# Window attention with fused mask-and-minimum sums, and the delta rule's decay rows from one pass over all chunks

## The reference, cut to what matters

```
G = jnp.cumsum(gc, axis=-1)
diff = G[..., :, None] - G[..., None, :]
dec_incl = jnp.where(incl, jnp.exp(jnp.where(incl, diff, 0.0)), 0.0)
...
t_mat = eye + bc[..., :, None] * dec_strict * kk
w_mat = triangular_solve(t_mat, ...)
```

```
s_loc = where(|i - j| <= 128, q k^T * scale, -1e30)
s_ctx = q k_ctx^T * scale
p = softmax(concat([s_loc, s_ctx, s_sink]))
o = p[..., :n_loc] v + p[..., n_loc:] v_ctx
```

## Time and profile before

| | |
|---|---|
| median of 3 executions | 3681.94 us (3679.02 to 3684.13) |
| the profiled execution | 3679.53 us, of which the span is 3677.7 us |
| PE busy | 3455.9 us (94% of the span) |
| DVE busy | 1802.4 us (49%) |
| ACT busy | 1175.1 us (32%) |
| POOL busy | 693.2 us (19%) |

### The profile page before, as it was taken

One profiled execution on the slowest core, in us unless ns is written; L12 is line 12 of the kernel. 1 busy time (PEld: TensorE's weight loads), 2 busy tenths in 40 slices (PEclk: granted clock), 3 DMA queues, 4 the chain that ended last, 5 costly groups with the idle time before them and its releaser, 6 DMA issues. The chain is left out here.

```text
span 3677.7 us, 49398 instructions
## 1 busy us (share of the span) xinstructions
PE 3455.9 (94%) x19822; PEld 2656.2 (72%) x19822; DVE 1802.4 (49%) x3343; ACT 1175.1 (32%) x2057; POOL 693.2 (19%) x528
## 2 busy tenths in 40 slices
PE   7999999999999999999976767988999999999998
PEld 6767778878888888875545656556887478888886
DVE  4277971233785554345577884678211243223222
ACT  3276751222211111234434453158111131112110
POOL 1190000110101111010020110048001213333333
PEclk9999999999999999999988887999999999999999
DMA  3101111121233322113012124000123011111111
GB/s 136 38 2 41 41 49 44 58 96 53 92 98 101 100 92 81 63 51 126 1 27 44 35 48 140 18 1 2 43 75 102 4 58 58 46 46 46 58 46 46
DMA packets 266352, 211.84 MB, mean 58 GB/s; under 512 B 65680, under 2 KB 231184, under 8 KB 265744
## 3 DMA queue, kind: packets, MB, share of 16 engines
q1 hardware_dynamic: 264368, 201.61, 17.7%
q10 hardware_dynamic: 1760, 7.08, 0.9%
HBM read 185.33 MB, written 21.50 MB: 56 GB/s over the span
## 5 line engine op out<-in xcount | busy, mean ns | idle before, releaser
L95 PE MATMUL ps<-halves 128*128 128x512 f32 x10408 | 2407.3, 392 | 18.4 <-DVE halves L1546 6.6
L95 PEld LDWEIGHTS ps<-halves 128*128 128x128 f32 x10408 | 1954.7, 188 | 441.3 <-issue 28.3
L95 PE MATMUL ps<-arena 128*128 128x512 f32 (+1 forms) x880 | 367.9, 572 | 8.0 <-issue 3.4
L1525 POOL TENSOR_TENSOR tmps<-tmps 128x512 f32<-128x512 f32 x128 | 143.9, 1124 | 979.6 <-ACT tmps L1493 979.6
L1546 DVE TENSOR_TENSOR halves<-tmps,halves 128x512 fp32r<-128x512 f32 x128 | 89.0, 698 | 432.2 <-ACT halves L1501 432.2
L1429 ACT ACTIVATE halves<-raws 128x2048 fp32r<-128x2048 f32 x62 | 118.4, 1909 | 554.8 <-PE ps L95 532.4
L95 PEld LDWEIGHTS ps<-arena 128*128 128x128 f32 x880 | 165.9, 193 | 168.4 <-issue 157.3
L1532 POOL TENSOR_TENSOR arena<-arena 128x512 f32<-128x512 f32 x128 | 164.7, 1294 | 191.4 <-DVE arena L1573 191.4
L1493 ACT ACTIVATE tmps<-ps 128x512 f32<-128x512 f32 x128 | 76.6, 598 | 363.7 <-PE ps L95 353.7
L1573 DVE TENSOR_TENSOR arena<-ps,arena 128x512 f32<-128x512 f32 x128 | 87.7, 690 | 194.9 <-PE ps L95 188.4
L1369 DVE SCALAR_TENSOR_TENSOR arena<-arena,sc 128x128 f32<-128x128 f32 x448 | 163.3, 365 | 15.9
(11 more groups left out here) (303 smaller groups left out, 3235.7 us busy)
## 6 DMA issues: line engine op xcount, KB each, us to landing
raws<-in_w_ff SPq DMA_DIRECT2D x31, 1024.0 KB, 6.7
raws<-in_w_mlp SPq DMA_DIRECT2D x31, 1024.0 KB, 5.2
mixw<-in_w_in SPq DMA_DIRECT2D x56, 512.0 KB, 3.8
arena<-in_w_ada SPq DMA_DIRECT2D x48, 512.0 KB, 3.9
arena<-in_w_in SPq DMA_DIRECT2D x5, 2048.0 KB, 12.0
arena<-in_x SPq DMA_DIRECT2D x8, 1024.0 KB, 8.4
h_stash<-arena SPq DMA_DIRECT2D x1, 5120.0 KB, 30.5
inverses<-arena ACTq DMA_DIRECT2D x20, 256.0 KB, 2.9
```

The lines of the kernel that those rows point to most:

```text
L95: ins = e.matmul(out_ap, l, r, start=i == 0, stop=i == n - 1)
L1525: e.tensor_tensor(tt, tt, tt, ALU.mult).then_inc(*f_sq.tick())
```

## The change

The change has two parts. **In the window attention** DVE's two mask additions, its copy and its two maxima become four fused instructions: each adds the mask (or a row of zeros for the context columns), writes the negated sum and keeps the minimum, which starts from the negated sink for the local columns and from the local minimum for the context columns. The comparison with the sink (L2893) goes, as does ACT's copy of head 1 (L2916). ACT's exponentials take the negated scores with scale -1. POOL scales head 0 only; DVE scales head 1, right behind its reciprocal. The last transposes of a unit wait for both. **In the delta rule** POOL's gate products go. In conv turn 6 instead of 9, PE makes the running sums of all blocks at once as rows (80 partitions, 256 columns, bank `("sr",)`); ACT and DVE split them into a high and a low part (`GH`, `GL`); SP writes both to DRAM and reads them back as 20 rows of 1024 each into `GR`, which POOL has zeroed; `tensor_decay_rows` then picks one row by a selector column of `E2`, with a float32r matmul in place of the float32 one. `scalar_decay_rows` takes over the waits that POOL had. The scratch `sq` of the conv stage moves to another place.

```diff
@@ -1785,6 +1785,9 @@
+            e.wait_ge(*b_ab.at(1))
+            e.tensor_copy(GC_.rearrange("p (d t h) -> p t d h", d=2, t=10),
+                          ga3.rearrange("p t (d h) -> p t d h", d=2)).then_inc(*b_ab.tick())
@@ -1792,7 +1795,7 @@
-        sq = R3(CB, 10, 128)
+        sq = R3(F0 + 14336, 10, 128)
@@ -1802,7 +1805,7 @@
-        DECAYS, CHUNK0 = 9, 9
+        DECAYS, CHUNK0 = 6, 9
@@ -1921,6 +1924,7 @@
+                    scalar_decay_parts(e)
@@ -2001,6 +2005,7 @@
+                    vector_decay_parts(e)
@@ -2048,7 +2053,13 @@
-        e_gg, e_sv, e_ex = C("delta_gates"), C("delta_small"), C("delta_small_exp")
+        e_gg, e_sv, e_ex = C("decay_parts"), C("delta_small"), C("delta_small_exp")
+        l_gr = LD("decay_rows")
+        g_rows = nc.dram_tensor("decay_rows", [2, 2, 10, 8, 128], F32, kind="Internal").ap()
+        GC_ = R(CB + 1072, 160)
+        E2 = RR[:, CB + 1664:CB + 1696]
+        GH, GL = RR[0:80, CB + 560:CB + 816], RR[0:80, CB + 816:CB + 1072]
+        GR = RR[:, CB + 2048:CB + 3072].rearrange("p (j s i) -> p j s i", j=4, s=2)
@@ -2085,6 +2096,43 @@
+            key = ("sr",)
+            o = bk.open(key, e_ev)
+            e.wait_ge(*bk.vacant(key))
+            e.wait_ge(*b_ab.at(3))
+            for dd in range(2):
+                ins = e.matmul(o[0:80, dd * 128:dd * 128 + 128], GC_[:, dd * 80:dd * 80 + 80], cum[:, dd, :], start=True, stop=True)
+            ins.then_inc(*bk.filling(key))
+        def vector_decay_parts(e):
+            e.tensor_tensor(E2, ident[:, 0:32], ident[:, 32:64], ALU.add).then_inc(*e_gg.tick())
+            e.wait_ge(*e_gg.at(2))
+            e.tensor_tensor(GL, bk.tile(("sr",))[0:80, 0:256], GH.bitcast(F32), ALU.subtract).then_inc(*bk.emptying(("sr",)))
+        def scalar_decay_parts(e):
+            e.wait_ge(*e_gg.at(1))
+            e.wait_ge(*bk.full(("sr",)))
+            e.activation(GH, bk.tile(("sr",))[0:80, 0:256], ACT.Copy).then_inc(*e_gg.tick())
+        def sync_decay_parts(e):
+            e.wait_ge(*bk.clear(("sr",)))
+            for part in range(2):
+                e.dma_start(g_rows[part].rearrange("d t h i -> (t h) d i"),
+                            (GH, GL)[part].bitcast(F32).rearrange("p (d i) -> p d i", d=2)
+                            ).then_inc(*l_gr.tick())
+            e.wait_ge(*l_gr.at(2))
+            e.wait_ge(*s_zero.at(1))
+            for part in range(2):
+                e.dma_start(RR[32 * part:32 * part + 20, CB + 2048:CB + 3072].bitcast(F32),
+                            g_rows[part].rearrange("d t h i -> (d t) (h i)")).then_inc(*l_gr.tick())
+        def gpsimd_decay_rows(e):
+            e.wait_ge(*bk.clear(("mask",)))
+            e.wait_ge(*bk.clear(("sg",)))
+            e.wait_ge(*bk.clear(("sr",)))
+            e.memset(RR[:, CB + 2048:CB + 3072].bitcast(F32), 0.0).then_inc(*s_zero.tick())
@@ -2113,26 +2161,16 @@
-        def gpsimd_gates(e, n, dd):
-            if n >= 10:
-                return
-            g = AB[:, ORDERS[dd][n], dd * 8:dd * 8 + 8].rearrange("p (j s) -> p s j", s=2)
-            if n >= 3:
-                e.wait_ge(*(bk.full(("so", n - 3, dd)) if latent(n - 3, dd) else bk.clear(("kk", n - 3, dd, 1))))
-            for s in range(2):
-                ins = e.tensor_tensor(IT[n % 3][dd][:, s * 4:s * 4 + 4, :], bc(g[:, s, :].unsqueeze(2), [P, 4, 128]),
-                                      bc(cum[:, dd, :].unsqueeze(1), [P, 4, 128]), ALU.mult)
-            ins.then_inc(*e_gg.tick())
         def tensor_decay_rows(e, n, dd, s):
-            e.wait_ge(*e_gg.at(turn[n, dd] + 1))
+            e.wait_ge(*l_gr.at(4))
-            chain(e, o[:, :], [(ones, IT[n % 3][dd][:, s * 4:s * 4 + 4, :]),
+            c = dd * 10 + ORDERS[dd][n]
+            chain(e, o[:, :], [(bc(E2[:, c:c + 1], [P, 128]), GR[:, :, s, :]),
@@ -2142,6 +2180,10 @@
+            if n < 3:
+                e.wait_ge(*bk.full(("ci", 11, 1024) if n else ("ci", 7, 512)))
+            else:
+                e.wait_ge(*(bk.full(("so", n - 3, dd)) if latent(n - 3, dd) else bk.clear(("kk", n - 3, dd, 1))))
@@ -2618,28 +2660,21 @@
         def gpsimd_delta(e):
-            e.wait_ge(*b_ab.at(2))
-            e.wait_ge(*l_cum.at(1))
-            e.wait_ge(*bk.full(("ci", 7, 512)))
-            for dd in BOTH:
-                gpsimd_gates(e, 0, dd)
+            gpsimd_decay_rows(e)
-            gpsimd_gates(e, 1, 0)
-            gpsimd_gates(e, 1, 1)
-                gpsimd_gates(e, n + 2, 0)
-                gpsimd_gates(e, n + 2, 1)
         def sync_delta(e):
+            sync_decay_parts(e)
@@ -2781,7 +2816,8 @@
-        w_mx, w_ex, w_rc, w_sl = C("watt_max"), C("watt_exp"), C("watt_recip"), C("watt_scaled")
+        w_mx, w_ex = C("watt_max"), C("watt_exp")
+        w_rc, w_sl = C("watt_recip_and_second_scaled"), C("watt_first_scaled")
@@ -2806,7 +2842,7 @@
-                            bk.open(key, w_et if key[0::2] == ("wc", 1) else w_es)
+                            bk.open(key, w_es)
@@ -2821,6 +2857,8 @@
+                        if c0 + n4 > nt:
+                            e.wait_ge(*w_rc.at(2 * u + 2))
@@ -2861,6 +2899,8 @@
         def vector_watt(e):
+            e.tensor_scalar(nsk, sk, -1.0, None, ALU.mult).then_inc(*dv.tick())
+            e.wait_ge(*dv.now())
@@ -2880,19 +2920,19 @@
-                        e.tensor_tensor(z[:, s, 0:nl], bk.tile(("wl", i, s))[:, 0:nl], wn[:, m0:m0 + nl],
-                                        ALU.add).then_inc(*bk.emptying(("wl", i, s)))
-                    e.wait_ge(*bk.full(("wc", i, 0)))
-                    e.tensor_copy(z[:, 0, nl:nl + 256], bk.tile(("wc", i, 0))[:, 0:256]
-                                  ).then_inc(*bk.emptying(("wc", i, 0)))
+                        e.tensor_tensor_reduce(out=z[:, s, 0:nl], in0=bk.tile(("wl", i, s))[:, 0:nl],
+                                               in1=wn[:, m0:m0 + nl], scale=-1.0, scalar=nsk[:, j + 4 * s:j + 4 * s + 1],
+                                               op0=ALU.add, op1=ALU.min, accum_out=c[:, 4 + s:5 + s]
+                                               ).then_inc(*bk.emptying(("wl", i, s)))
-                        e.wait_ge(*bk.clear(("wc", i, s)))
-                        e.tensor_reduce(c[:, s:s + 1], z[:, s, 0:nl + 256], AX.X, ALU.max,
-                                        negate=True).then_inc(*dv.tick())
-                    e.wait_ge(*dv.now())
-                    e.scalar_tensor_tensor(out=c[:, 0:2], in0=sk[:, j:8:4], scalar=-1.0, in1=c[:, 0:2], op0=ALU.mult,
-                                           op1=ALU.min).then_inc(*dv.tick())
-                    e.wait_ge(*dv.now())
+                        e.wait_ge(*bk.full(("wc", i, s)))
+                        e.wait_ge(*bk.clear(("wl", i, s)))
+                        e.tensor_tensor_reduce(out=z[:, s, nl:nl + 256].rearrange("p (a b) -> p a b", a=2),
+                                               in0=bk.tile(("wc", i, s))[:, 0:256].rearrange("p (a b) -> p a b", a=2),
+                                               in1=bc(wn[:, 128:256].unsqueeze(1), [P, 2, 128]), scale=-1.0,
+                                               scalar=c[:, 4 + s:5 + s], op0=ALU.add, op1=ALU.min,
+                                               accum_out=c[:, s:s + 1]).then_inc(*bk.emptying(("wc", i, s)))
+                    e.wait_ge(*bk.clear(("wc", i, 1)))
@@ -2901,20 +2941,15 @@
+                    n, j, lo, hi = watt_pair(u)
+                    p = pp_[u % 4][:, 1, 0:(hi - lo) * 128 + 256]
+                    e.wait_ge(*w_rc.at(2 * u + 1))
+                    e.tensor_scalar(p, p, c[:, 7:8], None, ALU.mult).then_inc(*w_rc.tick())
         def scalar_watt(e):
-                if i < 32:
-                    n, j, lo, hi = watt_pair(i)
-                    nl = (hi - lo) * 128
-                    if i >= 4:
-                        e.wait_ge(*watt_turned(i - 4))
-                    key = ("wc", i, 1)
-                    e.wait_ge(*bk.full(key))
-                    e.activation(pp_[i % 4][:, 1, nl:nl + 256], bk.tile(key)[:, 0:256],
-                                 ACT.Copy).then_inc(*bk.emptying(key))
@@ -2924,7 +2959,7 @@
-                                           accum_out=c[:, 2 + s:3 + s])
+                                           scale=-1.0, accum_out=c[:, 2 + s:3 + s])
@@ -2943,11 +2978,9 @@
-                e.wait_ge(*w_rc.at(i + 1))
-                for s in range(2):
-                    p = pp_[i % 4][:, s, 0:w]
-                    ins = e.tensor_scalar(p, p, w4[i % 4][:, 6 + s:7 + s], None, ALU.mult)
-                ins.then_inc(*w_sl.tick())
+                e.wait_ge(*w_rc.at(2 * i + 1))
+                p = pp_[i % 4][:, 0, 0:w]
+                e.tensor_scalar(p, p, w4[i % 4][:, 6:7], None, ALU.mult).then_inc(*w_sl.tick())

```

More of the change, by code:

```diff
@@ L2267, in sync_inverses @@
             if n == 0:
-                e.wait_ge(*s_zero.at(1))
+                e.wait_ge(*s_zero.at(2))
             for dd in range(2):
@@ L2393, in tensor_step_a @@
             else:
```

(4 more changed lines are left out.)

## The result

The changed kernel takes **3653.07 us** (median of 4 runs, 3647.21 to 3657.74) against 3683.03 (3679.02 to 3687.69): ratio 0.9917, 95% interval 0.9898 to 0.9937, so 23 to 38 us won and 30 in the middle. The forecast was 3662, the range 3652 to 3674. The time lies at the range's edge, on the fourth rival's value (3655), to which I had given 0.07: the turns of the window attention fell to PE's own length. The forecast's own range, 3655 to 3668, missed it by 2 us. So the direction was right and the likeliest case was not.

The account below looks back on a forecast made before the run. PE was taken to bound the conv stage, DVE the delta stage and window attention. Window attention 11.7 plus delta rule 8.1 gave 19.8 us off the profiled 3679.5, 2.4 under the median 3681.9: 3662, range 3652 to 3674.

Parts of the forecast that it names:

- the fourth rival: Window attention: the turns fall to PE's 3.78 us, 27 us won in all, time 3655; chance 0.07.
- DVE's turn falls by 0.36 to 3.95: Window attention: DVE loses 3.12 us a turn and gains 2.76; held by PE, 0.30 a turn is counted.
- The second rival: Window attention: fused instructions or DVE's scaling cost their upper ends, 0.68, 0.53 or 0.77; turns win nothing, 3672; chance 0.15.
- the prediction's lower bound: Window attention's worst case: 32 x (3.12 - 3.37) + 2.1, so 6 us lost.
- the turns of the eight smaller units I count alike: Window attention: the smaller units win the same per turn, so 32 x 0.30 = 9.6 us.
- The end: Window attention's end: POOL's last scaling finishes at 2566.8 instead of 2568.97, so mixing starts 2.1 us sooner.
- The detour's cost in the conv stage: Conv turn 6: two more float32 products on PE for the new rows cost 0.5 us; the rest is hidden.
- The second inverse: Delta stage: five DVE operations there shrink from 4.51 us to 1.3, 3.2 won.
- The later collisions: Delta stage, three later turns: DVE's first operations no longer collide with POOL, 3.1 us won.
- that rival: Delta stage: blocks through DRAM, not DVE, set the pace and the waits keep the gain; 3670; chance 0.10.
- 2.9 in sum, of which I take 2.3: Before the first delta block: L2251, L2248 and the pair L1964 are no longer stretched, 2.3 us counted.
- The port rival: Window attention: POOL's scaling, if first, shuts out DVE's for 1.87 us a turn; time 3722; chance 0.06.

Follow-up runs that it names:

- watt_alone: The kernel before with only the window attention's part of the change; 3661.18 us, ratio 0.9943.
- delta_alone: The kernel before with only the delta rule's part of the change; 3675.84 us, ratio 0.9976.
- the ten profiles: Profiles of kernels with the changed delta rule, two such kernels left out; mean delta stretch 600.1 us against 608.3 with the old rule.
- f32_product: The changed kernel with the decay product run as float32 instead of float32r; 3656.8 us.
- both_pool: The changed kernel with both heads' probability scalings back on POOL; 3661.1 us.
- first_and_last: The changed kernel with DVE scaling the second head only for the first unit and the last four, POOL for those between; 3656.5 us.
- late_rows: The changed kernel with the decay rows made in conv turn 9, right ahead of their first use, instead of turn 6; 3658.3 us.
- hybrid: The changed kernel with DVE scaling the second head only from unit 28 on, POOL before that; 3654.2 us.

## Why the prediction was right, and where it was wrong

**The window attention: 11.7 forecast, 20.8 measured.** The step that failed is "DVE's turn falls by 0.36 to 3.95", with the 0.30 a turn counted from it. The turn fell by 0.55, to 3.76. The next bound was named and sized rightly (PE's 3.78); what was too long is DVE's side. The four fused instructions take 1.88 and not 2.08: I had put the accumulator's read, 0.08 each, on top of the addition's time, and it overlaps the next instruction. The scaling costs 0.47 and not 0.58. Together 0.31 less, of which the own waits took 0.14 back (0.12 behind the last fused one and 0.12 ahead of the scaling, against 0.10). The second rival, the upper ends, falls by the same figures. (The 3.37 in the prediction's lower bound is more than its own terms give, 2 x 0.68 + 2 x 0.53 + 0.77 + 0.10 = 3.29; with that the bound is some 3 lost and not 6.) So DVE's turn ends at 3.765, in a tie with PE, and the fourth rival came about with DVE at its floor too. The second fault is "the turns of the eight smaller units I count alike" with nothing for the filling. There 17.2 us became 11.8. That DVE's and POOL's shorter work counts whole while the first three units pass through with nothing beside them is my reading, not tried by itself. PE's wait ahead of the first transposes shrank from 4.38 to the 1.72 shown above. The kernel before, PE there (timeline):

```profile
2441.17 1.94 PE L2826 MATMUL ps<-identm,arena 128*128 128x128 f32 x8 [4.38 <-DVE arena L2883]
2443.04 2.51 PE L2813 MATMUL ps<-arena 64*128 64x384 f32 x8
```

Those transposes took 1.94 instead of 1.07, the scores 2.51 instead of 1.69: PE's clock was down there. But the clock is not what the sum rests on: in `watt_alone` it fell behind the same wait of 1.72, and the window stretch is the same. Filling 5.4 and units 15.4 make the 20.8; between `delta_alone` and `watt_alone`, where the filling trades with the first turns, it is 2.4 and 17.6. The end was right, 2.1 forecast: from the last reciprocal's end to the mixing stage's first product 9.87 us became 8.05, 1.8 less (2564.72 to 2574.59, 2543.54 to 2551.59).

**The delta rule: 8.1 forecast, 7.0 in the profile of after, 8.2 over the ten profiles.** The sum was right, but by luck: two of its terms were off, one each way. The detour's cost in the conv stage, 0.5: 1780.06 to 1780.50, 0.44, and the first inverse begins 0.45 later. The second inverse, 3.2: the step from the second inverse's start to the third's fell from 40.2 to 36.9, 3.3, in all ten. The later collisions, 3.1: from the third start to the last, 262.9 became 258.5, 4.3 and so 1.2 more than forecast. The exchange through DRAM did not swallow them, so that rival falls. But "2.9 in sum, of which I take 2.3", ahead of the first and second block, came to 0.7: from the first inverse's start to the second's 51.5 became 50.8 on average (49.8 to 52.5 in the ten). By the third start the delta stage was 3.6 ahead, where I had named some 5. The stretched L2251 and L1964 did go. POOL's memset took the place of the first:

```profile
1879.86 3.52 POOL L2666 MEMSET arena<- 128x4096 f32 x1 [95.69 <-PE ps L95]
...
1880.07 0.26 DVE L2290 TENSOR_TENSOR arena<-arena 64x108 f32<-64x108 f32 x1
...
1882.06 1.86 DVE L1963 TENSOR_SCALAR arena<-arena,vec 128x1024 f32<-128x1024 f32 x1
1883.96 2.61 DVE L1968 SCALAR_TENSOR_TENSOR arena<-arena,vec 128x1024 f32<-128x1024 f32 x2
```

This is the kernel after (timeline). The memset waits for PE and begins at the same distance from the transposes as before (222.4); DVE reaches its scaling 1.0 us sooner, while the memset still runs, and the scaling takes 1.86 where the kernel before had 0.82 there. So it ends 226.5 behind the transposes in both. The pair behind it (L1964 before, L1968 after) keeps its gain, 2.61 instead of 3.92. Over the ten profiles the step is shortest, 49.8, where the scaling missed the memset (`f32_product`) and longest, 52.5, in the two where it was held longest (2.99 in `both_pool`, 2.84 in `first_and_last`); no kernel with the memset elsewhere was run. I had looked for what would be late next behind PE and DRAM, not behind the other instruction on POOL.

**The others.** PE's float32r product was rightly counted at nothing (`f32_product`), and the detour's cover was ample (`late_rows`). The port rival fell, by more than its condition: DVE started first by 0.06 in the changed kernel, as I had reckoned, and where POOL started first it cost DVE 0.25 in every second turn and the window stretch nothing. The rule of the Trainium skill, page "SBUF — State Buffer", section "Who interferes with whom", that the first holds the ports for its whole instruction, is borne out by the memset and not by POOL's scaling.

## What to carry to other kernels

When one engine's turn is shortened towards another's floor, work out both to the hundredth from start-to-start times, not from the durations shown: a read that overlaps the next instruction is no term of the sum. Cut the span at products that both kernels have; here the window stretch repeats within 0.4 us where the whole time scatters by 10. And when a contender on a shared engine goes, ask what that engine does next to it: much of the gain ahead of the second block went to a memset that had been harmless.

## What the runs showed of the hardware that I had not expected

POOL's memset holds a DVE scaling of 128x1024 until it ends. In 13 of the 14 profiles the scaling began while the memset ran, and in each it ended 0.54 or 0.55 us after the memset's end, whatever its start (0.82 to 2.99 us long). In `f32_product` alone it began after that, and took its 0.73:

```profile
1879.31 3.51 POOL L2666 MEMSET arena<- 128x4096 f32 x1 [93.99 <-PE ps L95]
...
1883.22 0.73 DVE L1963 TENSOR_SCALAR arena<-arena,vec 128x1024 f32<-128x1024 f32 x1
```

DVE's small products of two tensors ran through the same memset at their usual length (0.26 at 64x108 above, and 0.26 outside it), though they are what POOL's gate products stretch to 1.0. A POOL scaling that was under way held a DVE scaling for 0.25 at most; one that met a DVE scaling or the token subtraction was itself longer, 2.25 or 2.76 instead of 1.88. Why a memset holds the one and not the other, and why POOL's scaling lets go early, was not tried.

PE's granted clock was 0.50 behind a wait of 4.38 us at the filling in the kernel before, and 0.66 in the mean behind one of 2.97 in `hybrid`. Behind one of 1.72 it stayed at 1.00 in the kernel after, but in `watt_alone` it was 0.62 over the scores that follow. The wait's length alone doesn't decide it; what else does was not tried. What makes the unchanged stages ahead of the conv stage differ by 7 us from profile to profile was not tried either.
